# A two-layer hybrid diffusion backbone: norms between blocks in another order, and the first modulation as rows in two halves

## The reference

```python
sc = jax.nn.silu(c)                  # (1, 1024)
scc = jax.nn.silu(c_ctx)             # (1024,)
for l in range(DEPTH):               # 2
    sh1x, sc1x, ga1x, sh2x, sc2x, ga2x = jnp.split((sc @ w_mod[l] + b_mod[l])[:, None, :], 6, axis=-1)
    ...                              # the same from scc for the context tokens
    ux = rmsnorm(h, g_pre_mix[l]) * (1 + sc1x) + sh1x
    uc = rmsnorm(hc, g_pre_mix[l]) * (1 + sc1c) + sh1c
    yx, yc = token_mixers(ux, uc, ...)      # four kinds of attention, gates, w_out
    h = h + ga1x * rmsnorm(yx, g_post_mix[l])
    ux = rmsnorm(h, g_pre_ffn[l]) * (1 + sc2x) + sh2x
    h = h + ga2x * rmsnorm(swiglu(ux, w_ffn_in[l], w_ffn_out[l]), g_post_ffn[l])
    ...                              # the same for hc, but not in the last layer
return h
```

## Time and profile before

| | us |
|---|---|
| median of 3 runs | 1855.46 |
| lowest, highest | 1855.14, 1858.44 |
| the profiled execution | 1860.5 |
| its span in the trace | 1858.6 |
| PE busy | 1760.4 (95%) |
| DVE busy | 1153.9 (62%) |
| ACT busy | 883.1 (48%) |
| POOL busy | 584.6 (31%) |
| mean granted PE clock | 0.981 |

### The profile page before, as it was taken

How to read it: one execution, slowest core, us unless ns; L and a number is a source line. 1 busy time by engine, 2 the same in 40 slices (tenths; PEclk the granted TensorE clock), 3 DMA queues, 4 the chain that set the end, 5 groups by cost and what they waited for, 6 DMA issues and landing times. The chain is left out here.

```text
span 1858.6 us, 30522 instructions
## 1 busy us (share of the span) xinstructions
PE 1760.4 (95%) x10162; PEld 1491.9 (80%) x10162; DVE 1153.9 (62%) x2344; ACT 883.1 (48%) x1922; POOL 584.6 (31%) x555
## 2 busy tenths in 40 slices
PE   7999999999999999899999999788999999989998
PEld 3777888778788787788888888777898788979997
DVE  4356578677676765567777664456564456756655
ACT  4566555444344443542222223666565455565553
POOL 0354434455455452111111000124335655321100
PEclk8999999999999999999999999999999999999999
DMA  7222233344333235244556663233343323446664
GB/s 298 58 66 66 69 91 92 89 129 120 106 94 95 80 65 168 85 120 148 148 154 207 219 197 69 71 88 87 79 123 104 96 74 86 118 143 180 184 199 159
DMA packets 341254, 224.15 MB, mean 121 GB/s; under 512 B 57654, under 2 KB 322156, under 8 KB 340076
## 3 DMA queue, kind: packets, MB, share of 16 engines
q1 hardware_dynamic: 331692, 215.88, 41.0%
q10 hardware_dynamic: 9408, 6.32, 1.3%
HBM read 221.06 MB, written 1.07 MB: 120 GB/s over the span
## 5 line engine op out<-in xcount | busy, mean ns | idle before, releaser
L1946 PE MATMUL bank<-Uhi,w_ring 128*128 128x512 f32 (+1 forms) x1536 | 547.6, 357 | 18.2 <-ACT H L1628 7.4
L1947 PE MATMUL bank<-Ulo,w_ring 128*128 128x512 f32 (+1 forms) x1536 | 531.5, 346 | 0.0
L1948 PE MATMUL bank<-Uhi,w_ring 128*128 128x512 f32 (+1 forms) x1536 | 531.5, 346 | 0.0
L1488 ACT ACTIVATE w_ring<-load_ring 128x512 fp32r<-128x512 f32 (+3 forms) x632 | 370.0, 607 | 149.0 <-PE bank L1948 104.4
L1693 DVE TENSOR_TENSOR w_ring<-load_ring,w_ring 128x512 fp32r<-128x512 f32 (+1 forms) x424 | 319.6, 770 | 169.3 <-ACT w_ring L1488 150.3
L1946 PEld LDWEIGHTS bank<-Uhi,w_ring 128*128 128x128 f32 x1536 | 294.5, 192 | 59.8 <-ACT H L1628 10.5
L1948 PEld LDWEIGHTS bank<-Uhi,w_ring 128*128 128x128 f32 x1536 | 294.3, 192 | 36.3
L1443 POOL TENSOR_TENSOR w_ring<-load_ring,w_ring 128x512 fp32r<-128x512 f32 (+3 forms) x208 | 246.2, 1189 | 245.4 <-ACT w_ring L1488 140.7
L1947 PEld LDWEIGHTS bank<-Ulo,w_ring 128*128 128x128 f32 x1536 | 295.0, 192 | 29.8
L1431 POOL TENSOR_TENSOR Y<-Y,small 128x512 f32<-128x512 f32 x160 | 173.1, 1082 | 292.5 <-DVE small L1892 279.6
L1897 DVE TENSOR_TENSOR Z<-bank,Z 128x512 fp32r<-128x512 f32 x160 | 109.7, 686 | 96.2 <-ACT Z L1614 95.4
(11 more groups left out here) (142 smaller groups left out, 2661.8 us busy)
## 6 DMA issues: line engine op xcount, KB each, us to landing
load_ring<-in_w_in SPq DMA_DIRECT2D x192, 256.0 KB, 2.9
load_ring<-in_w_ffn_in SPq DMA_DIRECT2D x160, 256.0 KB, 3.1
mod_ring<-in_w_mod SPq DMA_DIRECT2D x96, 256.0 KB, 3.2
load_ring<-in_w_ffn_out SPq DMA_DIRECT2D x88, 256.0 KB, 3.4
mod_place<-in_w_mod SPq DMA_DIRECT2D x64, 256.0 KB, 2.8
load_ring<-in_w_branch SPq DMA_DIRECT2D x64, 256.0 KB, 2.9
mod_w<-in_w_mod SPq DMA_DIRECT2D x8, 1024.0 KB, 15.9
load_ring<-in_w_in SPq DMA_DIRECT2D x64, 128.0 KB, 2.5
```

The costliest lines, as they stand in the source:

```text
L1488: act.activation(w_ring[:, plan.slot['w', key], 0, 0:sz], load_ring[:, plan.slot['load', key], 0:sz], ACT.Copy).then_inc(sem['w_hi'], 1)
L1946: pe.matmul(dst, lhs[0], rhs[0], start=start, stop=False)
L1947: pe.matmul(dst, lhs[0], rhs[1], start=False, stop=False)
L1948: return pe.matmul(dst, lhs[1], rhs[0], start=False, stop=stop)
```

## The change

**The start.** PE makes all 2048 columns of the first modulation; DVE has no part in it. They are made in two halves: first columns 0 to 511 of shift and of scale (what the first 4 of the 8 input blocks need), then the others. The second half's row products stand between the first pieces of the first group: two blocks before piece 0, three before piece 1, three before piece 2. The weight is loaded as 16 DMAs of 512 KB. SP issues the tokens first, then the first half; `c`, `c_ctx`, the first constants and the 24 small DMAs are now issued by ACT, at the head of its list, ahead of its table load and its sigmoid. DVE takes a half of the tokens' norm and of their way out of PSUM (`un0d`, `xevd`).

**Between blocks.** `ysq` and `hsq` write to `tmp` in place of `fil`. The squares of the next tile's y stand before the squares of the last tile's h; the first of the two instructions of `ystat` is a step of its own (`ysum`) and is made long before. Both halves of the last product (`un_a`, `un_b`) are on DVE. `begin` treats the three last pieces with one transposition and one norm step for all four tiles, and goes through the blocks in the order in which the pieces use them: side 0 blocks 0 to 4, side 1 blocks 0 to 4, then 5 to 7. The transposition is always two blocks ahead of the product. `WARM` is 26.

```diff
-WARM = 22
+WARM = 26
...
-MOD0_DVE = 7 * P
-MOD0_ROWS = ((5, MOD0_DVE, 512), (6, MOD0_DVE + 512, 512), (7, MOD0_DVE + 1024, 128))
+MOD0_BANKS = ((5, 6), (3, 7))
...
     for tt in range(NTOK // P):
-        p.step('un0', tt)
-    for kt in (3, 4):
-        p.step('mod0', kt)
...
+        p.step('un0d' if tt % 2 else 'un0', tt)
+    first_rows(0, range(5))
     for l in range(DEPTH):
         p.take('acc', ('par', l), ('par_done', l))
         p.step('par', l)
...
+    turn_in(range(2))
+    first_rows(0, range(5, 6))
+    turn_in(range(2, 4))
+    first_rows(0, range(6, KT))
+    p.step('mod0row', 0)
+    turn_in(range(4, 6))
+    first_columns(0)
+    turn_in(range(6, KT))
+    first_rows(1, range(2))
...
                     p.step('apB', (nm, 0, kt - 1), side=None, cols=NTOK)
+                    first_rows(1, ((), (), (2, 3, 4), (5, 6, 7), (), (), (), (), ())[kt])
+                    if kt == 3:
+                        p.step('mod0row', 1)
+                    if kt == 4:
+                        first_columns(1)
+                        normed((nm, 0, kt), 0, 0, None, NTOK)
                     p.step('gmm', (first, kt - 1), side=0, both=False)
...
-            y_first(nmo, 1)
+            passes(1, 0, W_RING if nts > 2 else 1)
+            y_sum(nmo, 1, 1)
+            h_sum(nmo, 0, 0)
+            h_sum(nmo, 0, 1)
+            y_scale(nmo, 1)
+            p.step('hsum', (nmo, 0))
+            h_new(nmo, 1, 0)
+            p.step('hstat', (nmo, 0))
...
-            passes(3, 0, 3)
+            passes(3, 0, 2)
+            y_sum(nmo, 1, 2)
             u_next(nmo, 1)
-            passes(3, 3, W_RING)
-            return {(0, 0): [lambda: y_first(nmo, 3)], (0, 1): [lambda: h_next(nmo, 2)],
-                    (0, 3): [lambda: u_next(nmo, 2), lambda: h_next(nmo, 3)], (0, 5): [lambda: u_next(nmo, 3)]}
+            y_scale(nmo, 2)
+            passes(3, 2, 3)
+
+            def last(turn_first):
+                passes(3, 3, 4)
+                turn_first()
+                passes(3, 4, W_RING)
+
+            return {'last': [last],
+                    0: [lambda: h_new(nmo, 2, 0), lambda: y_sum(nmo, 1, 3), lambda: h_new(nmo, 2, 1)],
+                    1: [lambda: y_scale(nmo, 3), lambda: h_sums(nmo, 2), lambda: h_stat(nmo, 2)],
+                    2: [lambda: h_both(nmo, 3), lambda: u_next(nmo, 2)],
+                    3: [lambda: h_sums(nmo, 3), lambda: h_stat(nmo, 3)],
+                    4: [lambda: u_next(nmo, 3)]}
...
         @block.scalar
         def _(act):
+            act.dma_start(crows[0:8, 0, :], c.rearrange("b (k p) -> (b k) p", p=P)).then_inc(s_c, 16)
+            act.dma_start(crows[8:16, 0, :], c_ctx.rearrange("(k p) -> k p", p=P)).then_inc(s_c, 16)
+            act.dma_start(C[:, 0:NFIRST], consts[:, 0:NFIRST]).then_inc(s_first, 16)
+            for l in range(DEPTH):
+                act.dma_start(rows[0:48, l, :], b_mod[l].rearrange("(k p) -> k p", p=P)).then_inc(s_rows, 16)
...
             for kind, key, f in steps:
                 if kind == 'cin':
                     act.wait_ge(s_c, 32)
```

More of the change, by code:

```diff
@@ L317, in u_next, with begin @@
         p.step('un_b', (nmo, tt))
-    def begin(nm, l, which, first, nts, between):
-        def up_to(side, kt):
-            if kt < KT:
-                turn(nm, side, kt, range(2 * side, 2 * side + 2))
-        def ap(side, kt):
-            normed((nm, side, kt), l, which, side, SEQ, bank=('ut', nm, side, kt))
-            p.step('apB', (nm, side, kt), side=side, cols=SEQ)
-            for make in between.get((side, kt), ()):
-                make()
+    def begin(nm, l, which, first, nts, hooks):
         both = nts > 2
@@ L336, in begin, with turn_in, scale, low @@
         parts += [('gmm', 0, kt) for kt in range(W_RING, KT)]
-        tiles = [(side, kt) for side in range(1 + both) for kt in range(KT)]
-        ahead, made = 0, 0
-        for kind, side, kt in parts:
-            needed = tiles.index((1 if both and kind != 'gmm_a' else side, kt))
-            while ahead < min(len(tiles), needed + 3):
-                up_to(*tiles[ahead])
-                ahead += 1
-                if ahead > 1:
-                    ap(*tiles[made])
-                    made += 1
-            while made < min(len(tiles), needed + 2):
-                ap(*tiles[made])
-                made += 1
+        tiles = [(side, kt) for _, side, kt in parts]
+        whole = [both and kt >= W_RING for _, _, kt in parts]
+        def turn_in(i):
+            if i < len(tiles):
+                side, kt = tiles[i]
+                turn(nm, side, kt, range(NTOK // P) if whole[i] else range(2 * side, 2 * side + 2))
+        def scale(i):
+            if i < len(tiles):
+                side, kt = tiles[i]
+                turned_by(nm, side, kt)
+                normed((nm, side, kt), l, which, None if whole[i] else side, NTOK if whole[i] else SEQ,
+                       bank=('ut', nm, side, kt))
+        def low(i):
+            if i < len(tiles):
+                side, kt = tiles[i]
+                p.step('apB', (nm, side, kt), side=side, cols=NTOK if whole[i] else SEQ)
+                for make in hooks.get(i, ()):
+                    make()
+        scale(0)
+        for make in hooks.get('last', ()):
+            make(lambda: turn_in(0))
+        for i in (1, 2):
+            scale(i)
+            turn_in(i)
+            low(i - 1)
+        for i, (kind, side, kt) in enumerate(parts):
+            if i:
+                scale(i + 2)
+                turn_in(i + 2)
+                low(i + 1)
             p.step(kind, (first, kt), side=side, both=both)
@@ new lines, in output @@
+            y_sum(nmo, 1, 1)
+            h_sum(nmo, 0, 0)
+            h_sum(nmo, 0, 1)
+            y_scale(nmo, 1)
+            p.step('hsum', (nmo, 0))
+            h_new(nmo, 1, 0)
+            p.step('hstat', (nmo, 0))
+            if nts == 2:
+                passes(1, 1, 2)
+                h_new(nmo, 1, 1)
+                h_sums(nmo, 1)
+                u_next(nmo, 0)
+                h_stat(nmo, 1)
+                passes(1, 2, W_RING)
+                p.step('warm', nmo, times=WARM)
@@ L920, in output @@
                 u_next(nmo, 1)
[L921 to L924 removed]
+                return {'last': [lambda turn_first: turn_first()]}
+            h_new(nmo, 1, 1)
+            h_sums(nmo, 1)
             u_next(nmo, 0)
[L926 removed]
+            h_stat(nmo, 1)
             passes(2, 0, W_RING)
[L928 to L929 removed]
+            passes(3, 0, 2)
@@ new lines, in first_mod @@
+            def first_mod(h):
+                for k in range(KT):
+                    sp.dma_start(mod0_w[:, h, k], w_mod[0, k * P:(k + 1) * P, 0:MOD0].rearrange("p (a h m) -> p a h m", a=2, h=2)[:, :, h])\
+                        .then_inc(mod0_load[h][k], 16)
+            for i in range(2):
+                sp.dma_start(H[:, 2 * i:2 * i + 2, :], x_rows[i]).then_inc(s_x[i], 16)
+            first_mod(0)
+            for at, (what, key) in enumerate(plan.loads):
+                if at == L_RING:
+                    first_mod(1)
+                if what == 'consts':
@@ L2091, in _ @@
                         pe.wait_ge(sem[plan.lo[key]], count[plan.lo[key], key])
-                    parts = range(2) if kind == 'gmm' and both else (side,)
+                    parts = (side,)
                     for part in parts:
```

302 lines of the change are left out of this document (147 added, 155 removed).

## The result

The changed kernel was timed twice, each time beside the kernel before. First: 1859.99 us (median of 10, 1857.0 to 1865.4) beside 1856.13, ratio 1.0020 with a 95% interval of 1.0012 to 1.0029. Later, together with other kernels: 1859.19 beside 1860.11, ratio 1.0003 (0.9989 to 1.0017). The first timing says slower by 0.2%, the second tells no change; a gain of 0.17% (the forecast, 1852.3) lies outside both intervals. Ratios and medians can differ by some tenths of a microsecond to 1.5; where it matters, both are given. The profiled execution of the changed kernel took 1861.8, its span 1858.8, with PE busy for 1763.3 us and a mean clock of 0.986.

The account below looks back on a forecast made before the run. PE was taken as the bound nearly everywhere. Start +5.2, layer 0 places -3.0 and -1.1, layer 1 place -4.1 and tail -0.2 sum to -3.2, from 1855.5 to 1852.3 us; range 1845.5 to 1861.

Parts of the forecast that it names:

- The start, +5.2: Start through first group: `sc` ready at 13.6 behind 27 ACT issues, then 59.3 of gapless PE work, ending 72.9; +5.2 us.
- Rivals 1 and 2: Start: ACT issues small DMAs quickly, costing 2.1, chance 0.22; or they are held back, costing 10.8, chance 0.14.
- After the mixer of layer 1, -4.1: After layer 1's mixer: PE waits 1.6, stays warm, starts pieces at 1660.0 and ends at 1672.9; -4.1 us.
- the 2 that the prediction put for that case: After layer 1's mixer: if PE goes cold, the gain is only 2 us.
- signs of being wrong: Wrong if PE has gaps at the start, `sc` comes before 9 or after 17, or piece 3's wait is absent or over 7.
- under 2: After layer 1's mixer: the profile should show a PE wait under 2 us and no cold piece.
- The places of layer 0, -3.0 and -1.1: Layer 0: after the mixer, 803.1 against 806.09, -3.0 us; after the FFN, a late weight split leaves -1.1.
- 780.0: After layer 0's mixer: last tile normed at 780.0 against 785.77, read from ACT's list.
- The catch that the prediction named: After layer 0's mixer: transposition before piece 3 leaves PE idle from about 775.7 to 780.0; cold loss 2.2 us.
- Rival 3: Layer 0 places: transposition of tiles 2 and 3 stops PE longer, +2.9 at each, deciding from 782.9; chance 0.16.
- The tail, -0.2: Tail: the mean's first instruction leaves the last chain; -0.2 us.

Follow-up runs that it names:

- sig_first: Changed kernel with the first group's two sigmoids in layer 1's FFN moved ahead of the third block's pieces; 1856.70 us beside 1858.01 before, ratio 0.9992.
- pieces_first: Changed kernel with half pieces 3 and 4 of tiles 0 and 1 ahead of the transposition of tiles 2 and 3; 1855.93 us, ratio 0.9978 to before.
- small_spread: Changed kernel with small DMAs behind ACT's sigmoid and the norm of x, first half's row blocks before x's transposition, biases transposed later; 1855.82 us, ratio 0.9991 to before.
- c_first: As small_spread, but SP issues c, c_ctx and the first constants first, with two half row blocks ahead of x; 1859.09 us, ratio 0.9994 to before.

## Why the prediction was wrong

**The start, +5.2: right, by its own steps.** The issues took 10.4, `sc` came at 13.7, PE's work behind it was 59.5. Over all profiles with those starts stage 1 is 73.9 against 67.7 (five with the old start), +6.3. The execution that the forecast was read from was a slow one at this place (69.14, the four others 66.9 to 67.7), so part of the agreement with the timed +5.2 is luck. Rivals 1 and 2 (`sc` at 10.5 or 19.2) are refuted by the row at 13.51. The page "DMA: Bandwidth & Descriptors" of the Trainium skill, section "Issuing engines are not separate DMA queues", held here: what moved was sequencer time, and it stood ahead of `sc`. The drain that the page "ScalarE: Activation LUTs" of the Trainium skill, section "What ACT_TABLE_LOAD costs", adds to the load did not show: the sigmoid starts 12.46 - 11.16 = 1.30 after the start of the load, which lasts 1.28.

**After the mixer of layer 1, -4.1: the step that failed.** The local working came within 1 us (3.2) where the pieces began warm; where they began cold it was 1.0 instead of the 2 that the prediction put for that case. What failed is that its end was taken for the end of the account. I read the wait of 4.83 and never asked what a PE that arrives 3 to 4 us earlier meets next. It meets a sigmoid queued behind a split that waits for a load; stage 5, tail included, is 292.4 with the new norms (eight profiles) and 292.4 with the old (three with `WARM` 22). 4.1 of the forecast's sum were nothing, and sig_first shows that 2.7 of them can be had. No rival of the prediction named this, and none of its signs of being wrong looked beyond the places themselves: they came out as forecast or nearly so (a wait of 2.17 where "under 2" was said) while the total did not.

**The places of layer 0, -3.0 and -1.1: the first was too large.** Stage 3 is 493.5 against 495.6, -2.2 together instead of -4.1. Cut at the FFN's first matmul (the row at 808.99), the first place gives 0.8 and the FFN with the second 1.3, over nine profiles with the new norms and five with the old: the -3.0 is mis-sized, the -1.1 is not. The term that was mis-sized is DVE's part of tile 3's chain: 782.2 against 780.0, where I had followed ACT's list alone. 1.0 of it is the second half of tile 3's new h, made while POOL splits a weight; it is there in all twelve profiles with the new norms, and no run moved that split away. The catch that the prediction named, PE standing before piece 3, was real, and pieces_first shows that it cost over twice what the norms' new order had won (5.6 against 2.2). Rival 3 had this place and nearly its price: it decides from 782.9 on, and by its scale a tile 3 at 782.2 gives 0.7, where 0.8 was measured.

**The tail, -0.2,** is there in the rows (from the last tile's squares to its new h 2.33 before, 2.14 now) and below what can be timed.

Put together with the measured sizes: +6.3 for the start, -2.2 for stage 3 and 0 for stage 5 are +4.1. Stages 2 and 4, whose work on PE the change leaves alone, make it less: stage 2 is 2.0 shorter with the new start (626.6 in twelve profiles, 628.6 in five), stage 4 is 1.3 shorter with the new norms. Stage 4 varies from 368.3 to 373.7 within the old norms, so that is luck of single executions. Of stage 2's 2.0 us 0.5 belongs to the start: a wait of PE for DVE's `Z` near 400 us is 2.31 in all five profiles with the old start and 1.80 in all twelve with the new one. The rest comes from stretches behind waits, which the clock makes longer in one execution than in another, and stays open as a mean over so few. That gives +0.8 to +4.1, and the timings show +0.6 to +3.9.

## What to carry to other kernels

A gain at one place counts only after the next two queues have been read: ask what each engine has at the head of its list when the faster one arrives, above all an instruction that waits for a DMA ahead of one that frees a bank. Before an engine is made to stand for a late operand, put its work on early operands first, even if that bares a short latency behind. And DMAs cost time on the engine that issues them: none goes ahead of the first instruction that the start waits for.

## What I had not expected of the hardware

- With `c`, `c_ctx` and the constants issued on ACT at 0.74 to 2.13, while SP issues 2 MB of x and then the weights, the vectors were there at 6.05 and the constants at 8.44 (small_spread). Issued first on SP they were used at 2.60 and 3.45 (c_first). A small transfer on another engine's queue did not overtake large ones that were issued about the same time.
- The same instructions after a wait of 1.3 to 3.3 us in attention took, from execution to execution, one of two times 1.2 to 1.5 us apart, with the clock at its low level for some microseconds in one and not in the other (9.8 and 11.2 behind the wait of 2.04 at the last mark). Stage 4 goes from 368.3 to 374.0 through it, and from 370.8 to 374.0 between two profiles of one kernel. A place must be read from its own rows or from many profiles, not from the span of one.
- The second half of tile 3's new h on DVE (L1871) lasted 1.76 beside a weight split of POOL, and half of 1.41 before, without one. DVE shows no wait in either. In the kernel before, a low part on DVE at 779.00 took 0.97 instead of 0.41, beside POOL's split at 778.41. What couples the two engines was not tested.
